# Projection and second dense half: each block of x feeds both of the first two accumulations at once instead of the second two blocks later

## The chip, the cores and the metric

The kernel runs on one core of one Trainium2 chip. The metric is the device time of one execution in microseconds (us); of several executions the median is taken. TensorE is called PE in the rows (PEld is its loading of weights), VectorE DVE, ScalarE ACT, GpSimd POOL, SyncE SP.

## The reference, cut to what matters

The kernel is one step of a one-layer hybrid decoder on 1024 prompt tokens and 64 sample tokens (8 sequences of 8). Cut to the two stages that the change touches and what they stand in:

```python
def ffn_half_step(x, w_gate, w_up, w_down, g, b):
    return layer_norm(DEEP_ALPHA * x + 0.5 * swiglu(x, w_gate, w_up, w_down), g, b)
...
def swiglu(x, w_gate, w_up, w_down):
    return (jax.nn.silu(x @ w_gate) * (x @ w_up)) @ w_down
...
        xp = ffn_half_step(xp, ffn1_w_gate[l], ffn1_w_up[l], ffn1_w_down[l], ln1_g[l], ln1_b[l])
        q, k, v, qi, ki, wi, qkv, z, b_g, a_g = mix_projection(xp, w_in[l], pos_p)
        att = dsa_prompt(q, k, v, qi, ki, wi)
        gdn, s_new, c_new = gdn_branch(qkv, z, b_g, a_g, jnp.zeros((B, CONV_K - 1, GDN_CONV_DIM), xp.dtype),
...
        xp = mixer_residual(xp, att, gdn, w_o[l], ln2_g[l], ln2_b[l])
        xp = ffn_half_step(xp, ffn2_w_gate[l], ffn2_w_up[l], ffn2_w_down[l], ln3_g[l], ln3_b[l])
```

`mix_projection` is `h @ w_in` with 1024 rows in `w_in`, followed by rotary embedding. The model width is 1024, the hidden width of a dense half 2816.

## The kernel before, in words

**Stages.** The program is a row of stages, each a block that all engines enter and leave together: first dense half (`ffn`), projection (`project`), delta rule, index search, attention, output projection, second dense half (`ffn` again, now with `fresh` set). Activations stand transposed: 128 features on the partitions, 1092 token columns (1088 and four of padding) beside each other, in KT = 8 blocks of features. `x_hi` and `x_lo` are x split into two parts of lower precision; in the rows they are called `first_x_hi` and `first_x_lo` in the projection, `mixer_mix_hi` and `mixer_mix_lo` in the second dense half.

**A product.** `three_pass` multiplies a block of x by a block of weights of 128 x 128, three times (weights hi by x hi, hi by lo, lo by hi) over three slices of 364, 364 and 360 columns: nine matmuls for each k, written L86. Eight such blocks, k = 0 to 7, are one accumulation in PSUM. Two PSUM buffers alternate, `ps_a` and `ps_b`. An accumulation of 128 output rows is block n of the plan in the projection (28 of them: n = 0 is the indexer key `ki`), and gate or up of 128 hidden rows in the dense half (22 of each).

**The start of both stages.** The layer norm before a stage is finished inside it: for each k, VectorE scales a block of x (L1318 in the projection, L729 in the dense half), ScalarE makes `x_hi` (L1143, L531), VectorE makes `x_lo` (L1324, L735) and then counts `x_made` up. Between these VectorE also makes the low parts of the first weights (`weight_lo`, L1209 and L597), which count `wlo_done` up. While x comes, TensorE works on two accumulations, called a and b here after their buffers: in the projection blocks n = 0 and n = 1, in the dense half gate and up of the first 128 hidden rows. a0 to a7 and b0 to b7 are their eight products of nine matmuls. The loop of the dense half is

```python
                for step in range(KT + LAG):
                    if step < KT:
                        pe.wait_ge(s["x_made"], step + 1)
                        last = product("g", [step])
                        if step == KT - 1:
                            last.then_inc(gate_filled, 1)
                    if step >= LAG:
                        last = product("u", [step - LAG])
```

and that of the projection is the same with a wait for the second block's weights (`if step == LAG: pe.wait_ge(s["wlo_done"], 2)`) ahead of b0.

**What follows a7 in the projection.** When a7 is done (`filled` 1), ScalarE empties `ps_a` (`evacuate`, L1078) and makes the high part of the weights of block 2 (`weight_hi`, L1056). VectorE goes through its list: three parts of the rotary embedding of block 0 (L1247, L1254, L1257), the low part of the weights of block 2 (L1209), then the fourth part (L1260). TensorE waits for that low part (`wlo_done` 3) and for `ps_a` to be empty before it starts block 2.

**What follows a7 in the dense half.** When a7 is done (`gate_filled` 1), ScalarE takes silu out of `ps_a` (L509) and makes the high part of the next gate weights (L493), VectorE their low part (L597), and then, once b7 is done too, multiplies by up (L667). TensorE waits for silu and for that low part before it starts the gate of the second 128 hidden rows.

Of the kernel before, what the change touches and what calls it, by code (L numbers as in the profile page):

```python
# [189 lines left out]
    rstd: object  # L190


LAG = 2


def ffn(nc, name, w_gate, w_up, w_down, res, x_hi, x_lo, raws, ident, ones_mean, rstd_tok, rstd=None, weigh=False,
# [3 lines left out]
    with ExitStack() as ctx:  # L200
# [103 lines left out]
        def _(pe):  # L304
# [31 lines left out]
            def product(kind, ks):  # L336
                return three_pass(pe, ps_a if kind == "g" else ps_b, lambda k: hi[kind][:, k * P:(k + 1) * P],
                                  lambda k: lo[kind][:, k * P:(k + 1) * P],
                                  lambda k: x_hi[:, k], lambda k: x_lo[:, k], ks,
                                  start=0 in ks, stop=KT - 1 in ks)  # L340

            def gates_as_x_comes():
                pe.wait_ge(wlo_done["g"], 1)
                pe.wait_ge(wlo_done["u"], 1)
# [8 lines that stand above are left out]
                last.then_inc(up_filled, 1)  # L353
# [493 lines left out]
def project(nc, w_in, cos_in, sin_in, causal_in, conv_w, state_conv, a_log, dt_bias, ident, ones, x_hi, x_lo,  # L847
# [12 lines left out]
    with ExitStack() as ctx:  # L860
# [108 lines left out]
        def _(pe):  # L969
# [51 lines left out]
            def product(n, k):  # L1021
                last = three_pass(pe, ps[n % 2], lambda k: w_hi[:, n % 2, k * P:(k + 1) * P],
                                  lambda k: w_lo[:, n % 2, k * P:(k + 1) * P], lambda k: x_hi[:, k],
                                  lambda k: x_lo[:, k], [k], start=k == 0, stop=k == KT - 1)
                if k == KT - 1:
                    last.then_inc(s["filled"], 1)

            pe.wait_ge(s["pads_set"], 2)
            pe.wait_ge(s["wlo_done"], 1)
# [3 lines that stand above are left out]
                    product(0, step)  # L1033
                if step == LAG:
                    pe.wait_ge(s["wlo_done"], 2)
                if step >= LAG:
                    product(1, step - LAG)
# [2553 lines left out]
```

## Time and profile before

| | us |
|---|---|
| median of 3 runs | 3046.49 |
| lowest, highest | 3036.43, 3049.22 |
| the profiled execution | 3035.97 |
| its span, first to last instruction | 3034.3 |
| PE busy of the span | 2781.3 (92%) |
| DVE, ACT, POOL busy | 1538.5, 879.7, 275.2 |

The profile is of one execution; 1.7 us of its time lie around its span. Of its busy engines only PE comes near the span; a busy PE is not a PE at its peak, since its clock has two levels (1.00 is 2.4 GHz, 0.50 is 1.2 GHz). The projection begins at about 856 us of the span and ends at about 1293; the second dense half begins at about 2186 and goes on to the end.

### The profile page before, as it was taken

The numbers are of one execution on the slowest core, as the hardware profiler recorded it, in microseconds if no ns is written. First come the engines' busy times: TensorE is split into PE (matmuls) and PEld (weight loads), VectorE is DVE, ScalarE is ACT, GpSimd is POOL, SyncE is SP. The second block draws the span as 40 slices with busy tenths as digits, with TensorE's granted clock in tenths as the row PEclk, the third lists the DMA queues.
The fourth block names the chain that finished last, engine by engine and source line by source line (L and its number), as shares of the span: only waits on it lengthen the run. The fifth ranks groups of instructions, "written<-read, shape, count | busy, mean of one in ns | idle before, by whom it ended". The sixth has DMA issues, their size and how long they took to land. (4 is left out here: it accounts for less than half of the span.)

```text
span 3034.3 us, 44507 instructions
## 1 busy us (share of the span) xinstructions
PE 2781.3 (92%) x17285; PEld 2556.2 (84%) x17300; DVE 1538.5 (51%) x2426; ACT 879.7 (29%) x1450; POOL 275.2 (9%) x499
## 2 busy tenths in 40 slices
PE   6999999999989999968788788797889999999998
PEld 6999999999978799844688655467889999999998
DVE  5333333333465687837777578454453333333336
ACT  2111111111233557712355435352231111111113
POOL 0000000000510000005000000671000000000000
PEclk8999999999989999958899899898899999999999
DMA  3111111111232122224110101784011111111111
GB/s 110 56 42 43 43 42 43 42 49 49 63 84 65 50 73 72 86 86 113 42 53 12 54 15 33 205 234 132 28 42 49 43 42 43 49 43 42 46 39 60
DMA packets 262907, 190.96 MB, mean 63 GB/s; under 512 B 59503, under 2 KB 240959, under 8 KB 262694
## 3 DMA queue, kind: packets, MB, share of 16 engines
q1 hardware_dynamic: 207910, 106.27, 12.4%
q0 software_dynamic: 24096, 70.41, 7.2%
q10 hardware_dynamic: 30688, 11.27, 1.4%
q8 instruction: 153, 2.51, 0.3%
q14 instruction: 60, 0.49, 0.1%
HBM read 161.67 MB, written 26.22 MB: 62 GB/s over the span
## 5 line engine op out<-in xcount | busy, mean ns | idle before, releaser
L667 DVE TENSOR_TENSOR ffn_hidden<-ffn_hidden,ffn_ps_b 128x1092 f32<-128x1092 f32 x44 | 56.9, 1292 | 385.0 <-PE ffn_ps_b L86 385.0
L500 ACT ACTIVATE ffn_hi_d<-ffn_raw_d,ffn_row_mean 128x1024 fp32r<-128x1024 f32 x40 | 46.1, 1152 | 580.7 <-DVE ffn_row_mean L603 580.7
L516 ACT ACTIVATE ffn_h_hi<-ffn_hidden 128x1092 fp32r<-128x1092 f32 x44 | 49.2, 1119 | 483.4 <-DVE ffn_hidden L667 483.4
L251 POOL DMA_DIRECT2D ffn_raw_d<-in_ffn_w_down x40 | 21.3, 531 | 1569.9 <-DVE ffn_lo_d L612 1428.4
L86 PE MATMUL ffn_ps_a<-mixer_mix_hi,ffn_hi_g 128*128 128x364 f32 x528 | 119.2, 334 | 10.6 <-DVE mixer_mix_lo L735 8.0
L86 PE MATMUL ffn_ps_a<-first_x_hi,ffn_hi_g 128*128 128x364 f32 x528 | 118.2, 332 | 10.0 <-DVE ffn_lo_g L597 6.1
L86 PE MATMUL ffn_ps_a<-mixer_mix_lo,ffn_hi_g 128*128 128x364 f32 x528 | 117.5, 331 | 0.0
L86 PE MATMUL ffn_ps_a<-first_x_lo,ffn_hi_g 128*128 128x364 f32 x528 | 117.1, 330 | 0.0
L86 PE MATMUL ffn_ps_a<-mixer_mix_hi,ffn_lo_g 128*128 128x364 f32 x528 | 116.8, 330 | 0.0
L86 PE MATMUL ffn_ps_b<-first_x_lo,ffn_hi_u 128*128 128x364 f32 x528 | 116.6, 329 | 0.0
L86 PE MATMUL ffn_ps_a<-first_x_hi,ffn_lo_g 128*128 128x364 f32 x528 | 116.6, 329 | 0.0
L86 PE MATMUL ffn_ps_b<-first_x_hi,ffn_hi_u 128*128 128x364 f32 x528 | 116.5, 329 | 0.0
L86 PE MATMUL ffn_ps_b<-first_x_hi,ffn_lo_u 128*128 128x364 f32 x528 | 116.3, 328 | 0.0
L86 PE MATMUL ffn_ps_b<-mixer_mix_lo,ffn_hi_u 128*128 128x364 f32 x528 | 116.2, 328 | 0.0
L86 PE MATMUL ffn_ps_b<-mixer_mix_hi,ffn_hi_u 128*128 128x364 f32 x528 | 116.0, 328 | 0.0
L86 PE MATMUL ffn_ps_b<-mixer_mix_hi,ffn_lo_u 128*128 128x364 f32 x528 | 116.0, 328 | 0.0
L86 PE MATMUL ffn_ps_a<-ffn_h_hi,ffn_hi_d 128*128 128x364 f32 (+1 forms) x480 | 107.8, 333 | 5.5 <-DVE first_res L708 2.8
L509 ACT ACTIVATE ffn_hidden<-ffn_ps_a 128x1092 f32<-128x1092 f32 x44 | 47.6, 1082 | 218.5 <-PE ffn_ps_a L86 218.5
L2418 ACT ACTIVATE first_res<-main_scores_p,main_top_cand 128x768 bf16<-128x768 f32 (+2 forms) x96 | 99.0, 1034 | 33.2 <-DVE main_top_cand L2405 33.2
L86 PE MATMUL ffn_ps_b<-ffn_h_hi,ffn_hi_d 128*128 128x364 f32 (+1 forms) x480 | 106.3, 329 | 0.0
L86 PE MATMUL ffn_ps_a<-ffn_h_lo,ffn_hi_d 128*128 128x364 f32 (+1 forms) x480 | 105.5, 328 | 0.0
L86 PE MATMUL ffn_ps_b<-ffn_h_lo,ffn_hi_d 128*128 128x364 f32 (+1 forms) x480 | 105.5, 328 | 0.0
(714 smaller groups left out, 6930.4 us busy)
## 6 DMA issues: line engine op xcount, KB each, us to landing
ffn_raw_d<-in_ffn_w_down POOLq DMA_DIRECT2D x40, 512.0 KB
proj_raw<-in_w_in SPq DMA_DIRECT2D x22, 512.0 KB, 3.7
first_ffn_raw_g<-in_ffn_w_gate SPq DMA_DIRECT2D x21, 512.0 KB, 3.7
first_ffn_raw_u<-in_ffn_w_up SPq DMA_DIRECT2D x21, 512.0 KB, 3.8
second_ffn_raw_g<-in_ffn_w_gate SPq DMA_DIRECT2D x21, 512.0 KB, 3.9
second_ffn_raw_u<-in_ffn_w_up SPq DMA_DIRECT2D x21, 512.0 KB, 3.8
scratch_qkv<-first_res POOLq DMA_DIRECT2D x12, 544.0 KB, 3.0
delta_cur<-scratch_qkv SPq DMA_DIRECT2D x8, 768.0 KB, 5.4
```

What stands on the lines that cost most here:

```text
L86: last = pe.matmul(out[:, s, 0:USED[s]], w(k), x(k)[:, s * SL:s * SL + USED[s]], start=start and n == 0 and p == 0, stop=stop and n == len ...
L251: eng.dma_start(dst, src).then_inc(raw_in[kind], 16)
L500: act.activation(d_hi[:, k, :], raw["d"][:, :], ACT.Identity, bias=row_mean[:, k:k + 1]).then_inc(whi_done["d"], 1)
L509: act.activation(act_buf[:, fb, :].rearrange("p (s c) -> p s c", s=SLICES), ps_a[:, :, 0:SL], ACT.Silu).then_inc(silu_done, 1)
L516: act.activation(h_hi[:, par, fb, :], act_buf[:, fb, :], ACT.Copy).then_inc(hhi_done, 1)
L667: dve.tensor_tensor(hid, hid, ps_b[:, :, 0:SL], ALU.mult).then_inc(mul_done, 1)
L2418: act.activation(self.part(dump, i), self.score(i), ACT.Sign, bias=self.candidate(i), accum_out=self.count[:, i:i + 1]).then_inc(act_count ...
```

## The change

One constant becomes zero:

```diff
-LAG = 2
+LAG = 0
```

With it both loops run eight steps in place of ten, and in each step TensorE takes the block of x for a and then for b. In the projection the wait for the second weights now stands ahead of b0 in step 0. The instructions of all engines are the same in number and kind, and the order of VectorE, ScalarE, GpSimd and SyncE is the same; TensorE's order differs in these two places only.

TensorE at the start of the projection, from the end of a0, before (`[waits ...]` is what the row waits for; a semaphore that is used again stands under its first name in the program, so ffn1_hlo_done is `x_made` here and load_res_done `wlo_done`):

```order
L86 MATMUL proj_ps_a<-first_x_hi,proj_w_lo 128x364 x2
L86 MATMUL proj_ps_a<-first_x_hi,proj_w_lo 128x360
L86 MATMUL proj_ps_a<-first_x_hi,proj_w_hi 128x364 [waits ffn1_hlo_done]
L86 MATMUL proj_ps_a<-first_x_hi,proj_w_hi 128x364
L86 MATMUL proj_ps_a<-first_x_hi,proj_w_hi 128x360
```

and with the change:

```order
L86 MATMUL proj_ps_a<-first_x_hi,proj_w_lo 128x364 x2
L86 MATMUL proj_ps_a<-first_x_hi,proj_w_lo 128x360
L86 MATMUL proj_ps_b<-first_x_hi,proj_w_hi 128x364 [waits load_res_done]
L86 MATMUL proj_ps_b<-first_x_hi,proj_w_hi 128x364
L86 MATMUL proj_ps_b<-first_x_hi,proj_w_hi 128x360
```

After a0 comes b0, with a wait for the second weights, where a1 stood with its wait for x.

TensorE at the end of the two accumulations of the projection, up to the first matmul of block 2 (ffn1_mul_done stands for `evacuated`), before:

```order
L86 MATMUL proj_ps_b<-first_x_lo,proj_w_hi 128x360
L86 MATMUL proj_ps_b<-first_x_hi,proj_w_lo 128x364 x2
L86 MATMUL proj_ps_b<-first_x_hi,proj_w_lo 128x360
L86 MATMUL proj_ps_b<-first_x_hi,proj_w_hi 128x364 x2
L86 MATMUL proj_ps_b<-first_x_hi,proj_w_hi 128x360
L86 MATMUL proj_ps_b<-first_x_lo,proj_w_hi 128x364 x2
L86 MATMUL proj_ps_b<-first_x_lo,proj_w_hi 128x360
L86 MATMUL proj_ps_b<-first_x_hi,proj_w_lo 128x364 x2
L86 MATMUL proj_ps_b<-first_x_hi,proj_w_lo 128x360
L86 MATMUL proj_ps_a<-first_x_hi,proj_w_hi 128x364 [waits ffn1_mul_done,load_res_done]
```

and with the change:

```order
L86 MATMUL proj_ps_a<-first_x_lo,proj_w_hi 128x360
L86 MATMUL proj_ps_a<-first_x_hi,proj_w_lo 128x364 x2
L86 MATMUL proj_ps_a<-first_x_hi,proj_w_lo 128x360
L86 MATMUL proj_ps_b<-first_x_hi,proj_w_hi 128x364 x2
L86 MATMUL proj_ps_b<-first_x_hi,proj_w_hi 128x360
L86 MATMUL proj_ps_b<-first_x_lo,proj_w_hi 128x364 x2
L86 MATMUL proj_ps_b<-first_x_lo,proj_w_hi 128x360
L86 MATMUL proj_ps_b<-first_x_hi,proj_w_lo 128x364 x2
L86 MATMUL proj_ps_b<-first_x_hi,proj_w_lo 128x360
L86 MATMUL proj_ps_a<-first_x_hi,proj_w_hi 128x364 [waits ffn1_mul_done,load_res_done]
```

Between a7 and block 2 there were three products of b (b5, b6 and b7); now there is b7 alone.

TensorE at the same place of the second dense half, up to the gate of the second 128 hidden rows (its waits are for `silu_done` and `wlo_done` of the gate), before:

```order
L86 MATMUL ffn_ps_b<-mixer_mix_lo,ffn_hi_u 128x360
L86 MATMUL ffn_ps_b<-mixer_mix_hi,ffn_lo_u 128x364 x2
L86 MATMUL ffn_ps_b<-mixer_mix_hi,ffn_lo_u 128x360
L86 MATMUL ffn_ps_b<-mixer_mix_hi,ffn_hi_u 128x364 x2
L86 MATMUL ffn_ps_b<-mixer_mix_hi,ffn_hi_u 128x360
L86 MATMUL ffn_ps_b<-mixer_mix_lo,ffn_hi_u 128x364 x2
L86 MATMUL ffn_ps_b<-mixer_mix_lo,ffn_hi_u 128x360
L86 MATMUL ffn_ps_b<-mixer_mix_hi,ffn_lo_u 128x364 x2
L86 MATMUL ffn_ps_b<-mixer_mix_hi,ffn_lo_u 128x360
L86 MATMUL ffn_ps_a<-mixer_mix_hi,ffn_hi_g 128x364 [waits ffn1_silu_done,ffn1_wlo_done_g]
```

and with the change:

```order
L86 MATMUL ffn_ps_a<-mixer_mix_lo,ffn_hi_g 128x360
L86 MATMUL ffn_ps_a<-mixer_mix_hi,ffn_lo_g 128x364 x2
L86 MATMUL ffn_ps_a<-mixer_mix_hi,ffn_lo_g 128x360
L86 MATMUL ffn_ps_b<-mixer_mix_hi,ffn_hi_u 128x364 x2
L86 MATMUL ffn_ps_b<-mixer_mix_hi,ffn_hi_u 128x360
L86 MATMUL ffn_ps_b<-mixer_mix_lo,ffn_hi_u 128x364 x2
L86 MATMUL ffn_ps_b<-mixer_mix_lo,ffn_hi_u 128x360
L86 MATMUL ffn_ps_b<-mixer_mix_hi,ffn_lo_u 128x364 x2
L86 MATMUL ffn_ps_b<-mixer_mix_hi,ffn_lo_u 128x360
L86 MATMUL ffn_ps_a<-mixer_mix_hi,ffn_hi_g 128x364 [waits ffn1_silu_done,ffn1_wlo_done_g]
```

Here too one product of b is left between a7 and the next gate, where there were three.

## Rows read from the trace of the kernel before

**Rows 1.** The page: busy time of each engine, share of the span, instructions.

```profile
PE 2781.3 (92%) x17285; PEld 2556.2 (84%) x17300; DVE 1538.5 (51%) x2426; ACT 879.7 (29%) x1450; POOL 275.2 (9%) x499
```

**Rows 2.** Timeline of PE, projection: start, us, operation, count [idle before <-releaser].

```profile
866.25 1.11 PE L86 MATMUL proj_ps_a<-first_x_hi,proj_w_lo 128*128 128x364 f32 x3
867.15 1.11 PE L86 MATMUL proj_ps_a<-first_x_hi,proj_w_hi 128*128 128x364 f32 x3
...
870.45 0.76 PE L86 MATMUL proj_ps_a<-first_x_hi,proj_w_hi 128*128 128x364 f32 x3 [0.93 <-DVE first_x_lo L1324]
...
886.48 0.66 PE L86 MATMUL proj_ps_a<-first_x_hi,proj_w_lo 128*128 128x364 f32 x3
...
890.94 0.65 PE L86 MATMUL proj_ps_b<-first_x_hi,proj_w_lo 128*128 128x364 f32 x3
893.37 0.76 PE L86 MATMUL proj_ps_a<-first_x_hi,proj_w_hi 128*128 128x364 f32 x3 [1.78 <-DVE proj_w_lo L1209]
```

**Rows 3.** Timeline of DVE, projection, same columns.

```profile
866.64 1.22 DVE L1209 TENSOR_TENSOR proj_w_lo<-proj_raw,proj_w_hi 128x1024 fp32r<-128x1024 f32 x1
...
892.10 1.22 DVE L1209 TENSOR_TENSOR proj_w_lo<-proj_raw,proj_w_hi 128x1024 fp32r<-128x1024 f32 x1
```

**Rows 4.** Timeline of ACT, projection.

```profile
887.17 1.08 ACT L1078 ACTIVATE proj_xin<-proj_ps_a 128x1092 f32<-128x1092 f32 x1 [6.66 <-PE proj_ps_a L86]
```

**Rows 5.** Waits of PE, 893 to 1300 us: who for whom, total us, times, longest.

```profile
PE proj_ps_a L86 <- DVE proj_w_lo L1209: 6.1, 5, 2.4
```

**Rows 6.** Waits of DVE, the same stretch.

```profile
DVE proj_swapped L1247 <- ACT proj_xin L1078: 23.3, 8, 6.7
```

**Rows 7.** Timeline of PE, second dense half.

```profile
2192.41 1.25 PE L86 MATMUL ffn_ps_a<-mixer_mix_hi,ffn_hi_g 128*128 128x364 f32 x3 [8.00 <-DVE mixer_mix_lo L735]
...
2213.42 0.66 PE L86 MATMUL ffn_ps_a<-mixer_mix_hi,ffn_lo_g 128*128 128x364 f32 x3
...
2217.89 0.66 PE L86 MATMUL ffn_ps_b<-mixer_mix_hi,ffn_lo_u 128*128 128x364 f32 x3
2218.38 0.66 PE L86 MATMUL ffn_ps_a<-mixer_mix_hi,ffn_hi_g 128*128 128x364 f32 x3
```

**Rows 8.** Timeline of ACT and DVE, second dense half.

```profile
2193.45 1.36 DVE L735 SCALAR_TENSOR_TENSOR mixer_mix_lo<-second_res,second_gb,mixer_mix_hi 128x1092 fp32r<-128x1092 f32 x1
...
2195.98 1.36 DVE L735 SCALAR_TENSOR_TENSOR mixer_mix_lo<-second_res,second_gb,mixer_mix_hi 128x1092 fp32r<-128x1092 f32 x1
...
2214.11 1.08 ACT L509 ACTIVATE ffn_hidden<-ffn_ps_a 128x1092 f32<-128x1092 f32 x1 [5.36 <-PE ffn_ps_a L86]
...
2216.17 1.22 DVE L597 TENSOR_TENSOR ffn_lo_g<-second_ffn_raw_g,ffn_hi_g 128x1024 fp32r<-128x1024 f32 x1 [7.18 <-ACT ffn_hi_g L493]
```

**Rows 9.** Chain that ended last, in order of time: start, us, what.

```profile
2218.54 11.93 PE ffn_ps_a L86 x72
...
2242.52 1.30 DVE ffn_hidden L667
```

**Rows 10.** Timeline of PE: waits behind which the clock stayed, fell, or had fallen.

```profile
1203.62 0.30 PE L973 MATMUL proj_spare<-main_ident,main_k_t 128*64 128x128 f32 x1 [2.14 <-ACT proj_shared L1106]
...
2100.41 0.86 PE L86 MATMUL wo_ps_a<-mixer_mix_hi,wo_w_hi 128*128 128x364 f32 x3 [3.31 <-DVE wo_w_lo L3314]
...
2262.74 1.58 PE L333 MATMUL ffn_stat<-ffn_total,main_ones_mean 128*128 128x364 f32 x2 [13.14 <-DVE second_res L618]
```

**Rows 11.** Stretches: us from:to, length, busy (x count) by engine, PEclk, DMA share, GB/s.

```profile
864.00:868.40 4.40, 4.11 (x14) 4.14 (x15) 4.40 (x5) 2.06 (x2) 0.00 (x0) 0.50 1.07 289
868.40:872.00 3.60, 2.67 (x15) 2.37 (x14) 3.60 (x4) 1.51 (x2) 0.00 (x0) 0.96 0.72 179
...
1204.00:1210.00 6.00, 6.00 (x39) 5.98 (x38) 4.22 (x12) 5.88 (x11) 0.53 (x1) 1.00 0.41 141
...
2100.40:2104.40 4.00, 3.99 (x15) 3.99 (x16) 2.88 (x3) 1.06 (x1) 0.00 (x0) 0.57 0.42 119
...
2262.70:2268.20 5.50, 5.46 (x16) 4.92 (x17) 5.50 (x2) 0.00 (x0) 0.00 (x0) 0.50 0.14 56
```

## The prediction, as it was recorded before the changed kernel ran

> **What bounds the kernel now.** I read the page first: TensorE is busy for 92% of the span [rows 1], so what delays it in a stage without other slack delays the end. The change touches TensorE's order in two places of some 30 us each, so everything below is read from the timelines of those two places, and from the chain of work that ended last for what follows them. In full clock an accumulation of 72 matmuls takes 11.93 us [rows 9], so a product of nine takes 11.93 / 8 = 1.49 us. At half clock three matmuls follow the next three after 867.15 - 866.25 = 0.90 us [rows 2], so a product takes 2.70 us.
>
> In the projection TensorE waits once while x comes, 0.93 us ahead of a2 [rows 2]. From 870.45 us on it has work without a gap until b7 ends at 890.94 + 0.65 = 891.59. Then it waits 1.78 us for the low part of the weights of block 2, which is done at 892.10 + 1.22 = 893.32, and starts at 893.37 [rows 2, 3]. That low part is the last link of a chain that begins at a7: a7 ends at 886.48 + 0.66 = 887.14, ScalarE starts to empty its buffer at 887.17 [rows 2, 4], then come the next weights' high part and VectorE's list. From a7's end to the start of block 2 it is 893.37 - 887.14 = 6.23 us, of which b5 to b7 cover 4.45. So TensorE's wait is the open rest of a7's chain, and it is a7's end, not b7's, that sets when block 2 starts.
>
> In the second dense half TensorE starts at 2192.41 and runs through to the next gate at 2218.38 with no wait [rows 7]. Behind a7, which ends at 2213.42 + 0.66 = 2214.08, silu starts at 2214.11 and the next low part ends at 2216.17 + 1.22 = 2217.39 [rows 7, 8]: a chain of 3.31 us, which the three products b5 to b7 (4.47 us) hide, with some 1 us to spare. From there the chain that ended last runs over TensorE's gate and up into VectorE's multiplication at 2242.52 [rows 9], and on to a wait of 13.14 us that VectorE ends [rows 10].
>
> **The change part by part.** It adds no instruction and takes none away. It moves b's products forward among a's, so a7 is second to last in place of fourth to last: two products later against the end of the sixteen. That is 2 x 1.49 = 2.98 us for all that hangs on a7.
>
> Start of the projection: b0 now follows a0 and needs the second weights' low part, which ends at 866.64 + 1.22 = 867.86 [rows 3]. TensorE would be ready for it at 867.15 [rows 2], so it waits some 0.75 us there (started at about 867.91). The old wait of 0.93 us ahead of a2 goes, since a2 is now fifth in line and its x long there. What this makes of b7's end hangs on the clock. It is granted 0.50 until 868.4 and 0.96 in the stretch after that [rows 11], that is, the rise to 2.4 GHz comes near 868.7. If it rises then again, 0.8 us at half do 0.3 of a product and the other 14.7 take 21.9 us: all are issued at 890.6, with 0.3 us of tail b7 ends at 890.9, 0.7 us earlier than 891.59. If the new wait puts the rise off by as long as the 0.57 stretch behind another wait shows (a mean of 0.57 over 4 us is 3.4 us at half; at 1.49 to 2.70 they lose 3.4 x 0.45 = 1.5 us [rows 11]), b7 ends 1.5 us later than that, 0.8 us after 891.59. I take the middle: no change of b7's end, with both ends kept.
>
> So a7 ends 2.98 us later, and so does everything up to the start of block 2: +3.0 us (2.3 to 3.8). TensorE's wait ahead of block 2 grows from 1.78 to 1.78 + 2.98 = 4.8 us. Who is behind: SyncE's load of block 4's weights, which waits for the same low part, and they are needed two blocks on; and VectorE, which in the blocks that follow is itself waiting for ScalarE's emptying of PSUM (23.3 us in 8 waits [rows 6]), so it moves with TensorE and hides nothing.
>
> The clock after that wait: behind 2.14 us it stayed at 1.00; behind 3.31 us it showed 0.57 over the next 4 us, in which 15 matmuls ran in place of 4 / 0.166 = 24 (0.166 is 11.93 / 72), a loss of 9 x 0.166 = 1.5 us; behind 13.14 us it stood at 0.50 for 5.5 us [rows 10, 11], which by 1.49 to 2.70 loses 5.5 x (1 - 1.49 / 2.70) = 2.5 us. No row has 4.8 us in the same state, so its price lies between 0 and 2.5 us; by length the 3.31 us are nearest, and I take 1.5.
> The Trainium skill (TensorE: Matmul & The Clock Gate, HAM oscillation) has this as a rule against the change: a kernel whose matmuls come in bursts with long waits between them pays the slow start again behind each. By that rule the 1.5 us are there, and without it the sum below would be 5.1 in place of 6.6; the waits of 3.31 and 13.14 us agree with it, and that of 2.14 us shows a wait short enough to go free.
>
> Second dense half: TensorE's order while x comes costs nothing: a block of x comes every 2195.98 - 2193.45 = 2.53 us [rows 8], two products use it up in 2.98 us at full clock and more at half, and the clock starts low in either order. b7 ends where it did. a7 ends 2.98 us later, so the next low part ends at 2217.39 + 2.98 = 2220.37, and the next gate can start 0.05 us behind that, as block 2 does behind its low part (893.37 against 893.32 [rows 2, 3]): 2220.42 in place of 2218.38 [rows 7], +2.0 us. Behind a wait three matmuls take some 0.1 us more at first (0.76 against 0.66 us [rows 2]): +2.1 us. It is a wait that was not there, of some 2.1 us; the clock stays at such a length (2.14 us [rows 10, 11]), with 1.5 us as the upper bound. Queued behind it are gate and up of the second hidden rows. VectorE's multiplication of the first hidden rows now stands behind the later low part, so it moves too, but what needs its result ends the 11.93 us of gate later. The chain that ended last passes through this very gate and up [rows 9], so the end moves by the full 2.1.
>
> The sum is 3.0 + 1.5 + 2.1 = 6.6 us. Against the profiled execution it gives 3035.97 + 6.6 = 3042.6 us. The median of the runs shown is 10.5 us above that execution, so for the median I add the same sum: 3046.49 + 6.6 = 3053.1 us, 0.2% more.
>
> **The rivals.**
> 1. The clock does not fall behind the wider wait: 3.0 + 2.1 = 5.1, 3051.6 us. For it: the wait of 2.14 us; against it: that of 3.31.
> 2. The clock costs everywhere: late rise at the projection's start, long fall before block 2, a fall in the dense half: 3.8 + 2.5 + 2.1 + 1.5 = 9.9, 3056.4 us. For it: all four ends are within rows; against it: they would have to come together.
> 3. The projection gives its part back. TensorE also waits there later, 6.1 us in 5 waits for low parts of weights [rows 5]; if VectorE is late in those blocks for reasons of its own, the 4.5 us vanish into them, and 2.1 is left: 3048.6 us. Against it: VectorE waits for ScalarE's emptying in 8 places [rows 6], which hangs on TensorE.
> 4. Faster: what decides is the end of the sixteen products and not a7. The wait ahead of a2 goes, b7 ends 0.7 us earlier and block 2 follows it: 3046.49 - 0.7 = 3045.8 us. It decides only if the chain behind a7 is no longer than the one product now behind it, 1.49 us; it is 6.23 us in the projection and 3.31 in the dense half.
>
> **How the numbers follow.** Chances: the forecast 0.60, rival 1 0.15, rival 2 0.09, rival 3 0.11, rival 4 0.03, something unseen 0.02. All of them lie within 10 us of the median, while the three runs of before are 12.8 us apart; half a per cent, 15.2 us, is about what a measurement of this kernel can tell from no change. The range therefore comes more from the runs than from the rivals: the lowest run with the smaller sum, 3036.43 + 5.1 = 3041.5, and the highest with the larger, 3049.22 + 9.9 = 3059.1; I round to 3041 and 3060. The likeliest case's own range, without the spread of runs, is 3051 to 3055.5. Slower by over 0.5% needs rival 2 and a median at the upper edge of the runs: 0.07. Faster by over 0.5% needs a median below the lowest run shown: 0.03. The rest, 0.90, is within.
>
> **What would show it.** In the profile of the changed kernel, TensorE's rows should alternate between `ps_a` and `ps_b` product by product; the 0.93 us ahead of a2 are gone and a wait of about 0.75 us for a low part stands ahead of b0; block 2 starts about 6.2 us after a7's end, behind a wait of 4.8 us; the granted clock in the 5 us after it is well under 1.00; and the next gate of the dense half starts behind a new wait of about 2 us for its low part. The prediction is wrong if the wait ahead of block 2 stays under 2 us, if the next gate of the dense half starts right behind b7, or if the stage after the projection begins less than 2 us later than it did.

## The result, and the profile after

The changed kernel takes 3047.26 us (median of 20 runs, 3037.62 to 3055.90). The kernel before, run in turn with it, takes 3039.09 us (20 runs, 3034.02 to 3049.22). The ratio is 1.0023, with an interval of 1.0013 to 1.0033: the change costs 0.23%, or 7.0 us (4.0 to 10.0). The three runs that the prediction was based on had a median 7.4 us above that of the 20. The profiled execution of the changed kernel took 3050.06 us, with a span of 3048.4.

TensorE's timeline in the projection of the changed kernel, which answers to [rows 2]:

```profile
867.16 0.50 PE L86 MATMUL proj_ps_a<-first_x_hi,proj_w_lo 128*128 128x360 f32 x1
868.22 1.27 PE L86 MATMUL proj_ps_b<-first_x_hi,proj_w_hi 128*128 128x364 f32 x3 [0.56 <-DVE proj_w_lo L1209]
...
891.20 0.66 PE L86 MATMUL proj_ps_a<-first_x_hi,proj_w_lo 128*128 128x364 f32 x3
...
892.69 0.66 PE L86 MATMUL proj_ps_b<-first_x_hi,proj_w_lo 128*128 128x364 f32 x3
898.07 1.27 PE L86 MATMUL proj_ps_a<-first_x_hi,proj_w_hi 128*128 128x364 f32 x3 [4.73 <-DVE proj_w_lo L1209]
```

The wait of 0.93 us ahead of a2 is gone. A wait of 0.56 us for the second weights' low part stands ahead of b0. Only one product now stands between a7's last group (891.20) and the end of the sixteen (892.69 + 0.66 = 893.35), and the wait ahead of block 2 has grown from 1.78 to 4.73 us. ScalarE and VectorE show that the chain in between is the old one:

```profile
891.90 1.08 ACT L1078 ACTIVATE proj_xin<-proj_ps_a 128x1092 f32<-128x1092 f32 x1 [11.08 <-PE proj_ps_a L86]
```

```profile
896.80 1.22 DVE L1209 TENSOR_TENSOR proj_w_lo<-proj_raw,proj_w_hi 128x1024 fp32r<-128x1024 f32 x1
```

From a7's end (891.20 + 0.66 = 891.86) to block 2 it is 898.07 - 891.86 = 6.21 us, against 6.23 before. What TensorE's clock did is seen in the stretches of the changed kernel (from:to, length, busy and count of PE, PEld, DVE, ACT and POOL, then the granted clock, DMA share, GB/s):

```profile
868.20:873.40 5.20, 5.18 (x17) 5.18 (x18) 5.20 (x5) 2.41 (x2) 0.00 (x0) 0.50 0.74 167
873.40:890.00 16.60, 16.60 (x101) 16.60 (x100) 8.79 (x7) 3.64 (x3) 0.00 (x0) 1.00 0.00 1
...
898.07:907.60 9.53, 9.53 (x46) 9.08 (x47) 7.53 (x8) 6.80 (x8) 1.54 (x2) 0.50 0.46 154
907.60:915.00 7.40, 7.40 (x46) 7.40 (x45) 0.00 (x0) 0.00 (x0) 0.00 (x0) 1.00 0.61 186
2230.70:2232.70 2.00, 0.11 (x2) 0.06 (x1) 1.34 (x2) 0.63 (x1) 0.00 (x0) 1.00 0.02 4
2232.70:2240.00 7.30, 7.30 (x44) 7.30 (x45) 5.30 (x5) 6.18 (x6) 0.00 (x0) 1.00 0.45 129
```

The clock is at its lower level, 1.2 GHz, until 873.5: it rises 8.9 us after the projection's first matmul at 864.60, where it rose after 4.4 us before [rows 11]. Behind the wait ahead of block 2 it is at 1.2 GHz again for 9.5 us (10.2 us from its fall, which comes 0.7 us before the wait ends). In the dense half it stays at 2.4 GHz behind the new wait. That wait, in the timeline of all engines there:

```profile
2229.30 1.09 ACT L509 ACTIVATE ffn_hidden<-ffn_ps_a 128x1092 f32<-128x1092 f32 x1 [7.75 <-PE ffn_ps_a L86]
...
2230.09 0.66 PE L86 MATMUL ffn_ps_b<-mixer_mix_hi,ffn_lo_u 128*128 128x364 f32 x3
...
2231.36 1.23 DVE L597 TENSOR_TENSOR ffn_lo_g<-second_ffn_raw_g,ffn_hi_g 128x1024 fp32r<-128x1024 f32 x1 [9.57 <-ACT ffn_hi_g L493]
...
2232.64 0.77 PE L86 MATMUL ffn_ps_a<-mixer_mix_hi,ffn_hi_g 128*128 128x364 f32 x3 [1.89 <-DVE ffn_lo_g L597]
```

Silu starts 0.79 us before TensorE's last b product does its last group, where it had 3.8 us before [rows 7, 8]; so TensorE ends at 2230.75 and stands until 2232.64, 1.89 us. The chain that ended last in the changed kernel runs through this place:

```profile
2231.36 1.24 DVE ffn_lo_g L597
...
2232.64 12.20 PE ffn_ps_a L86 x72
2244.84 11.95 PE ffn_ps_b L86 x72
...
2256.89 1.30 DVE ffn_hidden L667
```

The two profiled executions differ by 3048.40 - 3034.31 = 14.1 us of span. The timelines divide this. The projection starts 0.3 later. From its first matmul to its last it takes 432.5 us where it took 423.6: +8.9. From there to the dense half it is 908.1 and 904.5: +3.6. From there to the end it is 843.2 and 841.9: +1.3. The 3.6 us lie in stages that the change doesn't touch, and a second profile of the kernel before has 909.6 us there, 5.1 more than its first (over the profiles of all runs it is 900.5 to 911.7): this part is within scatter. That leaves 10.2 us for the two places.

### The profile page after: what moved, and what is told of

It reads as the page before. It is cut to its first block and busy times, and to the rows that moved or that the text cites. A ratio compares the mean times of both kernels' runs of the same rounds, so it can differ in the third digit from the quotient of the medians.

```text
span 3048.4 us, 44522 instructions
## 1 busy us (share of the span) xinstructions
PE 2794.6 (92%) x17300; PEld 2564.5 (84%) x17300; DVE 1538.1 (50%) x2426; ACT 879.9 (29%) x1450; POOL 274.9 (9%) x499
```

## The experiments

The theory is that of the prediction: a7's place against the end of the sixteen products sets both waits. Its rivals are that the projection's part is given back, and that the end of the sixteen decides. The table has what was measured at the two places, in us, from the one profiled execution of each run. "a7", "block 2" and "block 3" are counted from the projection's first matmul, a7 to its end and the blocks to the start of their matmuls; "2 to 3" is from block 2's start to block 3's, which is 13.8 at full clock. "Multiplication" is the start of VectorE's second multiplication (line 667) after the dense half's first matmul.

| kernel | a7 | block 2 | its wait | block 3 | 2 to 3 | wait, dense half | multiplication |
|---|---|---|---|---|---|---|---|
| before | 22.84 | 29.08 | 1.78 | 42.89 | 13.81 | none | 50.10 |
| before, second profile | 22.83 | 29.07 | 1.78 | 42.88 | 13.81 | none | 50.50 |
| dense half alone | 22.83 | 29.07 | 1.78 | 47.35 | 18.28 | 1.89 | 51.68 |
| changed | 27.26 | 33.47 | 4.73 | 51.47 | 18.00 | 1.89 | 51.67 |
| changed, second profile | 24.87 | 31.09 | 4.73 | 48.94 | 17.85 | 1.89 | 54.57 |
| projection alone | 27.35 | 33.57 | 4.73 | 48.67 | 15.10 | none | 50.61 |
| lag 1 | 23.11 | 29.35 | 3.26 | 47.18 | 17.83 | 0.40 | 50.14 |
| lag 3 | 22.42 | 28.66 | 0.23 | 42.49 | 13.83 | none | 51.23 |
| lag 0, 24 filling matmuls | 26.83 | 33.08 | 4.76 | 46.90 | 13.82 | 1.89 | 54.27 |
| lag 0, 16 filling matmuls | 27.21 | 33.45 | 4.76 | 47.26 | 13.81 | 1.89 | 51.60 |
| lag 0, taps later | 26.88 | 33.09 | 4.73 | 49.40 | 16.31 | 1.89 | 54.32 |
| lag 0, low part first | 26.84 | 30.21 | 1.89 | 44.04 | 13.83 | 1.89 | 54.53 |
| lag 2, low part first | 22.85 | 27.15 | none | 40.87 | 13.72 | none | 50.55 |
| lag 1 and 2, low part first | 23.07 | 26.45 | 0.40 | 40.26 | 13.81 | none | 50.89 |
| lag 0, second low part early | 24.76 | 30.98 | 4.72 | 49.66 | 18.68 | 1.89 | 51.68 |
| the same, second profile | 24.83 | 31.04 | 4.72 | 49.76 | 18.72 | 1.89 | 54.68 |

With the filling, "its wait" is from b7 to block 2, with the filling in it.

**Each half alone.** The projection gets a constant of its own.

```diff
-LAG = 2
+LAG, LAG_P = 2, 0
...
-            for step in range(KT + LAG):
+            for step in range(KT + LAG_P):
```

> The lag is 0 in the projection alone, 2 in the dense half. Theory (a7's chain and the clock behind the wider wait, two thirds of the loss in the projection): block 2 starts 6.2 us after a7's end behind a wait of 4.7 us, the clock stands at 0.50 for some 5 to 10 us behind it, the dense half's second gate follows b7 without a wait, and the time is 5 to 8 us above the kernel before. Rival A (only the dense half's new wait costs, the projection's part is given back later): 0 us. Rival B (the loss is of the clock's level elsewhere and not of these places): anything, with no wait of 4.7 us.

It took 3044.86 us, ratio 1.0024 (1.0013 to 1.0034), +7.3 us: as expected, and rival 3 falls, since the projection's part reaches the end. The waits for low parts later in the projection say the same. In the changed kernel TensorE has, from block 2 on:

```profile
PE proj_ps_a L86 <- DVE proj_w_lo L1209: 9.1, 5, 4.7
```

Without block 2's own 4.7 that is 4.4 us in four waits; before it was 6.1 - 1.8 = 4.3 [rows 5]. Nothing vanished into them: from block 3 to the projection's last matmul it is 381.0 and 381.1 us in the two profiles of the changed kernel, 380.7 in both of the kernel before.

The other half, with `LAG, LAG_P = 0, 2`:

> The lag is 0 in the dense half alone, 2 in the projection. Theory: block 2 of the projection behind 1.8 us as before; the dense half's second gate starts behind a new wait of 1.9 us, silu 0.03 us behind a7's end, and the time is 2 us above the kernel before. Rival A: 7 us. Rival C (the dense half's 1.9 us vanish into the later wait of 13 us for VectorE): 0 us, and that wait is some 11 us.

It took 3043.25 us, ratio 1.0018 (1.0007 to 1.0028), +5.5 us (2.1 to 8.5): the expected 2 lies just below it, a miss by a little. The new wait is 1.89 us, and the multiplication comes 51.68 - 50.10 = 1.6 us later. The later wait of 13 us is still 13.1, so rival C falls; by the time alone rival A's 7 us would be possible too. But the projection, unchanged in it, showed something new behind its old wait of 1.78 us:

```profile
893.73 0.95 PE L86 MATMUL proj_ps_a<-first_x_hi,proj_w_hi 128*128 128x364 f32 x3 [1.78 <-DVE proj_w_lo L1209]
```

```profile
894.00:904.40 10.40, 10.40 (x51) 9.95 (x50) 7.24 (x8) 6.80 (x8) 1.54 (x2) 0.51 0.56 167
904.40:908.00 3.60, 3.60 (x23) 3.60 (x23) 0.00 (x0) 0.00 (x0) 0.00 (x0) 1.00 0.89 308
```

The clock fell for 10.2 us, and block 3 came 4.5 us late. The order of TensorE in the projection is that of the kernel before, so that kernel too can pay for its clock: in one of three profiles of this order it did. The two halves give 7.3 + 5.5 = 12.8 us against 7.0 for both. Each has some 3 us of interval to either side, so the difference of 5.8 is uncertain by about as much, and it stays open.

**Other lags.** With `LAG, LAG_P = 1, 1`:

> The lag is 1 in both places, so a7 is third to last. Theory (what counts is how many products stand behind a7): wait ahead of block 2 of 1.78 + 1.49 = 3.3 us, clock behind it lower or not by chance; dense half's second gate behind 0.4 to 0.5 us; time 2 to 5 us above the kernel before. Rival (it is the alternation of buffers that costs, not the place of a7): the waits as with lag 0.

3040.40 us, ratio 1.0001 (0.9989 to 1.0012): a miss, for +2 to 5 were expected. The table shows why: a7 is only 0.3 us later than at lag 2. At lag 1 the sixteen products themselves end 1.2 us earlier (b7 at 26.09 in place of 27.30), because neither x nor the second low part is waited for, and the place that a7 lost is won back at the start. The wait ahead of block 2 is 3.26 us, but its growth of 1.5 us is nearly all b7's earlier end. In this profile the clock fell behind it, for 10.2 us, and block 3 came 4.3 us later than in the kernel before. The median of 12 runs shows nothing of these 4.3 us; how often the clock falls there was not measured.

With `LAG, LAG_P = 3, 3`:

> The lag is 3 in both places, so a7 is fifth to last. Theory: wait ahead of block 2 of 0.3 us in place of 1.8, but one more wait for x of about 1 us ahead of a3, so block 2 starts 0.4 us earlier; the dense half loses some tenths on x and has no wait at its second gate; time within 1 us of the kernel before. Rival (a7 earlier is worth 1.5 us each): 1.5 us below.

3037.75 us, ratio 1.0001 (0.9992 to 1.0011), as expected. The wait is down to 0.23 us, but TensorE waits 0.62 and 0.77 us for x instead and b7 ends 1.1 us later, so block 2 starts only 0.4 us earlier. A shorter wait alone is no gain: a7's end is what counts, and it moved by 0.4.

**The clock behind the wait.** At lag 0, filling matmuls behind b7 write to a spare buffer that nothing reads before it is written again, so that TensorE is busy for most of the wait.

```diff
+                if n == 1 and k == KT - 1:
+                    for r in range(FILL):
+                        last = pe.matmul(spare[:, 0, 0:SL], w_hi[:, 1, 0:P], x_hi[:, r % KT, 0:SL], start=True, stop=True)
```

> Lag 0 in both places, and behind b7 of the projection TensorE runs 24 more matmuls of 364 columns into a buffer that nobody reads before it is overwritten (they add work, the outputs are the same). Theory (part of the loss is the clock that falls in the wait of 4.7 us): the matmuls fill some 4 us of that wait, block 2 starts as late as with lag 0, but the clock behind it stays at 1.00, and the time is 2 to 4 us below that of lag 0, 3 to 5 above the kernel before. Rival (the clock costs nothing there): as lag 0, 7 us above the kernel before.

At its place it did what was expected: the clock stays at 1.00, and block 3 follows block 2 in 13.82 us, where it was 18.00 in the changed kernel. The total did not: 3053.47 us, ratio 1.0048 (1.0033 to 1.0063), +14.6 us. The excess stands 1.7 ms later: from VectorE's second multiplication to the end this profile has 806.0 us, the other fifteen 790.3 to 793.6. It lies in the loop of the second dense half, in waits for which the profile shows no cause ("issue"). TensorE's waits in that half, with 24 filling matmuls:

```profile
PE ffn_ps_a L86 <- issue: 8.2, 6, 2.2
```

```profile
2559.98 0.76 PE L86 MATMUL ffn_ps_a<-mixer_mix_lo,ffn_hi_g 128*128 128x364 f32 x2 [2.25 <-issue]
```

The changed kernel has 2.5 us in three such waits, the longest 0.9. Three of the six here last about 2 us, from 2557.7, 2708.1 and 2858.1 on, and behind each the clock is low for 6.8 us, which by 1.49 against 2.70 us for a product loses 3.0 us: 3 x (2 + 3) = 15 us. To see whether the length of the program does it, the same filling was made of 16 wider matmuls (`FILL = 16`, 512 columns):

> As the run with 24 more matmuls behind b7 of the projection, but with 16 of 512 columns, so that TensorE's program is longer by 32 instructions and not by 48. Theory (the 14 us lost with 24 came from the place of the second dense half's loop in TensorE's program, not from the matmuls): the gaps of some 2 us inside that loop are gone, the clock stays at 1.00 through block 2, and the time is 2 to 4 us below lag 0. Rival (the added matmuls themselves cost, by heat or power): again some 14 us above the kernel before, with gaps in the loop or a lower clock there.

3044.41 us, ratio 1.0014 (1.0006 to 1.0023), +4.3 us (1.8 to 7.0): as expected, though the interval overlaps that of lag 0 (4.0 to 10.0). TensorE's filling and the stretch behind the wait:

```profile
891.09 3.86 PE L1028 MATMUL proj_spare<-first_x_hi,proj_w_hi 128*128 128x512 f32 x16
896.01 0.77 PE L86 MATMUL proj_ps_a<-first_x_hi,proj_w_hi 128*128 128x364 f32 x3 [1.06 <-DVE proj_w_lo L1213]
```

```profile
896.00:905.00 9.00, 8.99 (x67) 8.73 (x68) 7.53 (x8) 6.80 (x8) 1.53 (x2) 1.00 0.44 144
```

The waits of 2 us in the later loop are gone (4.4 us in six, the longest 0.9). This fits the theory that the number of instructions ahead of the loop matters to it, but the two fillings differ in the matmuls' width too, and each has one profile. The trace's DMA packets point the same way. The queue q8 carries instructions, and in the stretch from 2557.6 to 2560 us of the run with 24 it has the only packet of all queues (packets, MB, share of the 16 engines' time):

```profile
q8 instruction: 1, 0.02, 2.3%
```

Such a packet starts at 2557.65, 2707.47 and 2857.75, at most 0.6 us ahead of each of the three long waits, and each wait ends 1.3 to 1.5 us after the packet's end. In each of the sixteen profiles three such packets stand some 3.5 us apart at these turns of the loop, where most in the loop stand some 21 us apart. So the loop's code was being fetched as TensorE waited; that TensorE waited for it is likely, but no run took the fetch away.

The other suspicion was that the 24 small transposes behind the first product of block 2 keep the clock low. They were moved behind the block's last product, at lag 0 (the taps are the helper's name for them):

```diff
-    if n == 2 and k == 0:
+    if n == 2 and k == KT - 1:
         return [("taps", 0)]
```

> Lag 0 in both places, and the 24 small transposes of the convolution's weights stand behind the last product of block 2 in place of the first. Theory (the small transposes, of 4 and 24 columns, right behind the wait keep the clock from rising): the clock is at 0.50 for some 3.5 to 5.5 us behind the wait in place of 9.5, and block 3 starts 1 to 2 us earlier than with lag 0. Rival (the small transposes have no part): 9 to 10 us at 0.50, as with lag 0.

3048.69 us, ratio 1.0030 (1.0020 to 1.0039), +9.1 us. The clock was low for 6.8 us in place of 10.2, where 3.5 to 5.5 were expected, and block 3 came 16.3 us behind block 2 in place of 18.0. But with the projection alone at lag 0, the transposes in their old place, it was low for 3.4 us and block 3 came after 15.1, and the total here is no lower. One profile each doesn't show that the transposes are the cause.

**The wait itself.** VectorE does the rotary embedding of the block just emptied ahead of the next low part. Here the low part of block 2's weights goes first, in both lags:

```diff
+                    if n == 1:
+                        weight_lo(n + 1)
                     block_work(n - 1, range(3))
-                    if n + 1 < n_blocks:
+                    if 1 < n < n_blocks - 1:
                         weight_lo(n + 1)
```

At lag 0:

> Lag 0 in both places, and VectorE makes the low part of block 2's weights ahead of block 0's rotary embedding in place of behind three parts of it. Theory (VectorE's list is what makes a7's chain long): the chain behind a7 shrinks from 6.2 to 3.3 us or less, the wait ahead of block 2 from 4.7 to 1.9 us, the clock stays at 1.00, and the time is 4 to 7 us below lag 0, 0 to 3 above the kernel before. Rival (ScalarE's emptying of the buffer, with its follower, is what TensorE waits for): the wait ahead of block 2 stays over 3 us.

At lag 2:

> The kernel before (lag 2) with the low part of block 2's weights ahead of block 0's rotary embedding. Theory: the chain behind a7 of 3.3 us or less fits under the three products behind it (4.5 us), the wait of 1.8 us ahead of block 2 is gone, and the time is 1 to 2 us below the kernel before. Rival (the delayed rotary embedding holds up block 1's emptying and gives it back): no change.

At lag 0 it took 3042.91 us, ratio 1.0012 (1.0003 to 1.0021), +3.6 us, just above the expected 0 to 3. The chain from a7 is cut from 6.21 to 3.38 us, block 2 starts behind a wait of 1.89 us and the clock stays up, so the theory holds and the rival falls. At lag 2 it took 3032.14 us, ratio 0.9983 (0.9973 to 0.9994), -5.2 us (1.8 to 8.2): faster than both kernels. The low part is ready before b7 ends, and block 2 follows at once. In its timelines of VectorE and TensorE:

```profile
888.01 1.23 DVE L1209 TENSOR_TENSOR proj_w_lo<-proj_raw,proj_w_hi 128x1024 fp32r<-128x1024 f32 x1 [7.28 <-ACT proj_w_hi L1056]
```

```profile
889.72 0.66 PE L86 MATMUL proj_ps_b<-first_x_hi,proj_w_lo 128*128 128x364 f32 x3
890.21 0.66 PE L86 MATMUL proj_ps_a<-first_x_hi,proj_w_hi 128*128 128x364 f32 x3
```

Block 2 starts 1.9 us earlier than before. For the time 1 to 2 us were expected, and the gain is larger. Part of the rest can be the clock: there is no wait left there, and in one of the three profiles with the old order it had fallen behind that wait; this was not measured. With lag 1 in the projection, lag 2 in the dense half (`LAG, LAG_P = 2, 1`) and the low part first:

> Lag 1 in the projection, 2 in the dense half, and VectorE makes the low part of block 2's weights ahead of block 0's rotary embedding. Theory: lag 1 frees TensorE of its wait for x ahead of a2 without a wait for the second weights, b7 ends 1.2 us earlier than with lag 2, and the chain behind a7 (3.4 us) just fits under two products (3.0 us) and a wait of some 0.4: block 2 starts 0.3 to 0.8 us earlier than with lag 2 and the same move, 2.2 to 2.7 us earlier than in the kernel before, and the time is 5 to 6 us below it. Rival (a clock that rises later eats it): as the kernel with lag 2 and the same move.

3036.90 us, ratio 0.9990 (0.9981 to 0.9999), -3.0 us (0.3 to 5.8). Block 2 starts 2.6 us earlier than before, as expected, but for the time 5 to 6 us were expected, and it is not told apart from that of lag 2.

**Second profiles.** The two kernels once more, unchanged:

> The kernel before once more, for a second look at its clock behind the wait of 1.8 us ahead of block 2. Theory (there it falls in some executions and in others not): either block 3 starts 13.8 us after block 2 with the clock at 1.00, or some 18 us after it with the clock at 0.50 for about 10 us. Rival (it never falls there with the kernel's own program): 13.8 us.

> The changed kernel once more, for a second look. Theory: wait of 4.7 us ahead of block 2 and of 1.9 us ahead of the dense half's second gate again; the clock behind the first is at 0.50 for 3 to 10 us (block 3 starts 15 to 18 us after block 2), behind the second by chance for 3.4 us. Rival (the clock behind the first wait falls in some executions only): block 3 starts 13.8 us after block 2.

They took 3041.80 and 3053.82 us, one execution each. The waits ahead of block 2 and of the second gate are the same to 0.01 us. In the kernel before the clock again stayed up behind its wait. In the changed one it rose 2.9 us after the projection's first matmul in place of 8.9, so a7 ended 2.4 us earlier, and in the dense half it fell behind the new wait:

```profile
2236.10 0.77 PE L86 MATMUL ffn_ps_a<-mixer_mix_hi,ffn_hi_g 128*128 128x364 f32 x3 [1.89 <-DVE ffn_lo_g L597]
```

```profile
2237.20:2240.60 3.40, 3.40 (x13) 3.40 (x13) 2.21 (x3) 3.32 (x4) 0.00 (x0) 0.50 0.56 159
```

Of nine profiles with lag 0 in the dense half, the clock fell there in five, each time for 3.4 us, which by 1.49 against 2.70 us loses 1.5. In those five it had risen 5.3 to 6.2 us after the half's first matmul; in the four others 2.8 to 3.0.

**The short wait at the start.** What was open by then was why a7 is 4 us late at lag 0 where two products make 3. The second weights' low part is made directly behind the first, so that b0 has nothing to wait for:

```diff
             weight_lo(0)
+            weight_lo(1)
...
-                if k == 1:
-                    weight_lo(1)
```

> Lag 0 in both places, and VectorE makes the low part of the second block's weights right behind that of the first, ahead of x_lo of k = 1, so that b0 of the projection finds its weights ready. Theory (the wait of 0.56 us ahead of b0 puts off the clock's rise): no wait ahead of b0, the rise comes 3 to 5.6 us after the first matmul as with lag 2, a7 ends some 25 us after the first matmul in place of 27, block 2 starts 2 us earlier than with lag 0, and the time is 2 us below lag 0, 5 above the kernel before. Rival (the alternation of the products puts it off): the rise 8 to 9 us after the first matmul and a7 at 27 us though b0 does not wait.

> The same kernel for a second look, since the rise comes at another time in each execution. Theory: rise again 3 to 5.6 us after the first matmul. Rival: 8 to 9 us.

In both profiles the wait of 0.56 us is gone, the clock rises 4.5 and 4.7 us after the first matmul, and a7 ends at 24.8 us. With the short wait the rise came after 8.0 to 9.2 us in six of seven profiles (a7 at 26.8 to 27.4), and after 2.9 in one (a7 at 24.9). In the nine profiles without it, whatever the lag, it came after 2.8 to 5.6. So the wait goes with a late rise, and the alternation of the products, which stayed, does not. But the clock, which falls within block 2's wait, was now low for longer, 13.7 us, of which 11.1 lie behind the wait:

```profile
892.60:906.30 13.70, 11.08 (x51) 10.63 (x52) 10.11 (x11) 6.80 (x8) 1.53 (x2) 0.50 0.45 139
```

Block 3 came 18.7 us behind block 2, and the total is 3048.24 us, ratio 1.0032 (1.0021 to 1.0044), +9.7 us where +5 was expected; the execution of the second profile took 3042.99. What was won at the start did not reach the end, and why the low stretch lasts 13.7 us here is open.

## Why the prediction was right in its sum, and where it was wrong

**The mechanism was right.** All that it named to look for is there: the alternating products, a wait of about 0.75 us ahead of b0 (0.56), 6.2 us from a7 to block 2 (6.21), a wait of 4.8 us (4.73), a low clock behind it, and a wait of about 2 us ahead of the next gate (1.89). Rival 4, that the end of the sixteen decides, falls with lag 3 and lag 1: there b7 ended 1.1 us later and 1.2 us earlier, and block 2 followed a7 by 6.24 us both times. Rival 3 falls with the projection alone. Rival 1, no fall of the clock, is seen in none of the six profiles with lag 0 in the projection and the wait of 4.7 us left bare. Of rival 2, the clock everywhere, each piece was seen; all three together in one profile, that with the taps later.

**The step that failed** is the one on the measurement: "half a per cent, 15.2 us, is about what a measurement of this kernel can tell from no change". It was taken from the spread of three runs. Medians of 20 runs each gave an interval of 0.1%, 3 us and not 15, to either side, so +0.23%, 7.0 us (4.0 to 10.0), is a slowdown that can be told, and the forecast sum of 6.6 us should itself have said so; instead 0.90 went to "within" and 0.07 to slower. The size lies inside the half per cent, but a change of this size was not beyond measuring. The same three runs put the base at 3046.49, 7.4 us too high. The time of 3053.1 is 5.8 us too high: the base by 7.4, while the sum of 6.6 is too low by 1.6 if the two medians are subtracted (8.2), and by 0.4 by the ratio (7.0). The likeliest case's own range, 3051 to 3055.5, misses 3047.26, which lies in the wide range of 3041 to 3060.

**The terms**, by means over the profiles in the table:
- a7's later end, 3.0 forecast (2.3 to 3.8): 26.75 us (seven profiles at lag 0 with the short wait) against 22.84, +3.9. Two products' places are in it as reckoned. The rest is b7's end, taken as unchanged with 0.8 us later as the upper end: the late rise is the usual case and not one end of the range. In the changed kernel's first profile it made b7 end at 28.75 in place of 27.30, 1.45 later, for the clock rose 4.5 us later; without the short wait b7 ended some 1.0 us earlier than before.
- The clock behind the wait, 1.5 forecast (0 to 2.5): in the three profiles of the same order in the projection (both of the changed kernel, and the projection alone) 4.2, 4.0 and 1.3 us over the 13.8 us from block 2 to block 3, mean 3.2. The upper end of 2.5 was taken from 5.5 us of low clock behind 13.14 us; here 9.5 us of it stand behind 4.73. But the order of the kernel before pays as well: 0, 0 and 4.5, mean 1.5. The difference of 1.7 is close to the forecast by luck: both sides were larger than thought. The forecast took [rows 10, 11] as a list of waits by length, in which 1.78 us is free; the profile of the dense half alone shows that it is not always.
- The dense half, 2.1 forecast: 53.2 (nine profiles) against 50.5 us (five at lag 2), +2.7. The wait itself costs what was forecast, and this shows where the clock rose at nearly the same time, 6.0 and 6.2 us after the half's first matmul: the second gate starts at 28.80 us at lag 0 (changed, second profile) and at 26.75 at lag 2 (lag 1 and 2, low part first), 2.05 later. In the changed kernel's first profile the difference looks smaller, 1.45, because its clock rose after 2.9 us and that of the kernel before after 4.1. What was costed at nothing, with 1.5 as the upper bound, is the clock behind the wait: in five of nine profiles it paid that bound. Those five had a late rise at the half's start, but so had the profiles at lag 2 (4.1 to 6.2 us), so the late rise is no cost of the change here.

Projection to block 3 (49.7 against 44.4, three profiles each) and dense half make 5.3 + 2.7 = 8.0 us, inside the 4.0 to 10.0 that were measured. These are means over few executions, and the single ones lie several us apart. The Trainium skill's rule (TensorE: Matmul & The Clock Gate, HAM oscillation), that bursts of matmuls with long waits between them pay the slow start again, is borne out behind the 4.73 us, at 0.50 for 9.5 us.

Open remain: what sets the length of the low stretch behind block 2's wait (3.4 to 13.7 us from fall to rise, in one and the same order of instructions or nearly so), why the taps moved and the second low part moved gave nothing in the total, and how often each of these falls of the clock comes in executions that were not profiled.

## What to carry to other kernels

Two accumulations that share a stream of inputs want the first to finish early if its result heads a long chain: count the work that stands behind the last product of the first, and compare it with the chain, 6.2 us here against one product of 1.5 us. Where a wait remains, shorten the chain and not the wait, by putting first in the waited engine's list what TensorE needs next; that made the kernel 5.2 us faster where interleaving the products cost 7.0. And before calling a change too small to tell, reckon the interval of the medians that will be measured, not the spread of a few runs.

## What the runs showed of the hardware that was not expected

- The clock's fall behind a wait was not set by the wait's length alone. In the projection it fell behind 1.78 us in one of three profiles and stayed in two; in the dense half it fell behind 1.89 us in five of nine, those in which it had risen 5.3 to 6.2 us after the half's first matmul and not 2.8 to 3.0.
- With a wait of 0.56 us some 3 us after the first matmul the clock rose only after 8.0 to 9.2 us in six of seven profiles; without it, after 4.5 and 4.7.
- In the profile with 24 more matmuls in straight code, a loop 1.7 ms later lost about 14 us, in three waits of some 2 us with a fetch of instructions at their start and 6.8 us of low clock behind each; with 16 wider ones it did not.
